# Two token tiles normalised together in the transition of a gated mixer with a grouped mixture of experts

## The chip, the cores and the metric

The kernel runs on one NeuronCore of a Trainium2 chip. The metric is the device time of one execution in microseconds (us), as the median of several runs. A NeuronCore has TensorE (matrix products and transposes, with weight loads of their own), VectorE, ScalarE, GpSimd and SyncE, each with its own queue of instructions that is worked in order. The engines wait for one another by semaphores. TensorE reads SBUF and writes PSUM, whose eight banks hold 512 float32 columns each.

## The reference, cut to what matters

There are 512 tokens of width 1024 and one layer, all in float32. The first half mixes tokens and ends in `w_out`; the second half sends each token to two of 16 experts. Between the two stands a norm:

```python
x = x + g_m * (merged @ w_out)                        # residual
hf = rmsnorm(x, norm_ffn_g) * (1 + sc_f) + sh_f       # norm and modulation
logits = hf @ router_w                                # 16 experts
probs = softmax(logits); best group of 4, best 2 experts in it
x = x + g_f * grouped_moe(hf)                         # gate, up, down of the chosen experts
out = rmsnorm(x, final_norm_g)
```

`rmsnorm(x, g)` is `x * rsqrt(mean(x * x) + 1e-6) * g`, for each token.

## The kernel before, in words

Tokens lie on the 128 partitions, in four tiles (`NT = 4`). Every wide product is made of three, in float32r, from operands split into a high and a low part (`three`, L1203 to L1205). ScalarE makes the high part, VectorE the low part (`lo`, L684); for the first two expert chunks GpSimd makes the low part (L448). A stage of products with `w_out` is followed by the transition, and that by the expert stage, in which expert tiles of up to 128 gathered rows run through one loop. The expert stage starts only when the router's choice is known: VectorE ranks the experts, TensorE and VectorE turn the choice into row numbers, GpSimd gathers rows from a copy of `hf` in DRAM.

The transition is the part that the change touches. The order of each engine's work there is written out by hand:

- **TensorE** finishes `w_out` for tile t in two halves of 512 columns (PSUM bank `4 - 4 * half + t`), tile by tile. After the last half it transposes the normed tiles 0 and 1 (`turn_normed`, L1411), makes the router's logits of both (`logits`, L1400), then transposes tile 2, makes its logits, and the same for tile 3. The transposes of tile t wait for `hf_ready` above t.
- **VectorE** does for each half `mixed(t, half)`: it waits for that half of `w_out`, multiplies it in PSUM by the gate row (L923) and adds `x` into SBUF (L926, `x2_half`). `normed(t)` waits for the sum of squares (`sq2`), takes an inverse root of one column in ten small instructions (`inv_rms_1`, L719 to L729) and scales the tile (L932, `hf_scaled`). The order is: residuals of tile 0, norm 0, residual 1 first half; then, for t from 1 to 3: second half of t, first half of t + 1, norm of t. Last it adds the shift to tile 3 (L956), after GpSimd has added it to tiles 0 to 2 (`hf_ready` at least 3).
- **ScalarE** squares and sums tile t when both halves of its residual are there (L604), and copies transposes from PSUM to SBUF as the router's operand (`turned`, L230). It squares tiles 0, 1, 2, copies transposes 0 and 1, squares tile 3, and copies transposes 2 and 3.
- **GpSimd** adds the shift to tiles 0 to 2 as each is scaled (L454).
- **SyncE** saves each finished tile of `hf` to DRAM (L337), and when all are saved and transposed starts three weight loads for the experts.

`inv_rms(col, n)`, used elsewhere in the kernel for four columns at once, is an inverse root for n columns in twelve dependent small instructions (L695 to L707). After each the engine waits for its end. The loop that orders residuals and norms is:

```python
            for t in range(1, NT):
                mixed(t, 1)
                if t < NT - 1:
                    mixed(t + 1, 0)
                normed(t)
```

Of the kernel before, what the change touches and what calls it, by code (L numbers as in the profile page):

```python
# [15 lines left out]
NT = SEQ // P  # L16
# [28 lines left out]
def tokens_moe_kernel(nc, A, out):  # L45
# [18 lines left out]
    with ctx:  # L64
# [41 lines left out]
        with nc.sbuf_tensor("hT", [P, 2, ND, SEQ], F32R) as hT:  # L106
# [56 lines left out]
        sq2, hf_scaled, hf_ready, hf_saved, hf_t, hfT_ready, logits_mm, expd, mask_ready, pos_mm, tiles_ready = map(  # L163
            sem, ("sq2", "hf_scaled", "hf_ready", "hf_saved", "hf_t", "hfT_ready", "logits_mm", "expd", "mask_ready",
                  "pos_mm", "tiles_ready"))
# [58 lines left out]
        def turned(act, activation, t):  # L224

            for half in range(2):
                act.wait_ge(hf_t, 2 * t + half + 1)
                if t >= 2:
                    act.wait_ge(logits_mm, t - 1)
                activation(hfT[:, t % 2, 4 * half:4 * half + 4, :].rearrange("p k m -> p (k m)"),  # L230
                           ps[:, 5 * (t % 2) + half, :], ACT.Copy).then_inc(hfT_ready, 1)
# [251 lines left out]
        def _(act):  # L483
            A_ = nc.scalar.activation
# [112 lines left out]
                hi(c + 2, c + 2, 16 * (RAW_O // 4 + 2), G0 + 16)  # L597

            for t in range(NT):
                if t == NT - 1:  # L600
                    turned(act, A_, 0)
                    turned(act, A_, 1)
                act.wait_ge(x2_half, 2 * t + 2)
                A_(hf[:, t, :], x_tiles[:, t, :], ACT.Square, accum_out=stats[:, 24 + t:25 + t]).then_inc(sq2, 1)  # L604
            for t in range(2, NT):
                turned(act, A_, t)
            act.wait_ge(sub_ready, 1)
            A_(r_p, r_d, ACT.Exp).then_inc(expd, 1)
# [61 lines left out]
        def _(dve):  # L670
# [3 lines left out]
            def step(ins):  # L674

                steps[0] += 1
                ins.then_inc(chain, 1)

            def done():
                dve.wait_ge(chain, steps[0])  # L680
# [10 lines left out]
            def inv_rms(col, n):  # L691

                m, yv, sq = stats[:, col:col + n], nrm[:, 0:n], nrm[:, NT:NT + n]
                yi, mi = nrm[:, 0:n].bitcast(I32), m.bitcast(I32)
                step(V.tensor_scalar(m, m, 1.0 / D, EPS, ALU.mult, ALU.add))  # L695
                done()

                step(V.tensor_scalar(yi, mi, 1, None, ALU.logical_shift_right))
                done()
                step(V.tensor_scalar(yi, yi, -1.0, float(0x5F3759DF), ALU.mult, ALU.add))  # L700
                done()
                for last in (False, False, True):
                    step(V.tensor_tensor(sq, yv, yv, ALU.mult))
                    done()
                    step(V.scalar_tensor_tensor(out=sq, in0=sq, scalar=-0.5, in1=m, op0=ALU.mult, op1=ALU.mult))
                    done()
                    step(V.scalar_tensor_tensor(out=m if last else yv, in0=sq, scalar=1.5, in1=yv,  # L707
                                                op0=ALU.add, op1=ALU.mult))
                    done()

            def inv_rms_1(col):


                m, z = stats[:, col:col + 1], nrm[:, 0:1]
                zi = z.bitcast(I32)
                powers = [nrm[:, NT + j:NT + j + 1] for j in range(3)]
                for j in range(3):
                    f = 4.0 ** (3 - j)
                    step(V.tensor_scalar(powers[j], m, f / D, f * EPS, ALU.mult, ALU.add))  # L719
                done()  # L720

                step(V.tensor_scalar(zi, powers[2].bitcast(I32), -0.5,
                                     float(0x5F3759DF - (2 << 23) - (1 << 31)), ALU.mult, ALU.add))
                done()
                for j in range(3):
                    step(V.scalar_tensor_tensor(out=nrm[:, 2 * NT:2 * NT + 1], in0=z, scalar=powers[j], in1=z,  # L726
                                                op0=ALU.mult, op1=ALU.mult))
                    done()
                    step(V.scalar_tensor_tensor(out=m if j == 2 else z, in0=nrm[:, 2 * NT:2 * NT + 1],  # L729
                                                scalar=-3.0, in1=z, op0=ALU.add, op1=ALU.mult))  # L730
                    done()
# [188 lines left out]
            def residual(t, half):  # L920

                b = 4 - 4 * half + t
                step(V.tensor_tensor(ps[:, b, :], ps[:, b, :], gm[:, half * 512:half * 512 + 512], ALU.mult))  # L923
                done()
                x_h = x_tiles[:, t, half * 512:half * 512 + 512]
                V.tensor_tensor(x_h, ps[:, b, :], x_h, ALU.add).then_inc(x2_half, 1)  # L926

            def normed(t):

                dve.wait_ge(sq2, t + 1)  # L930
                inv_rms_1(24 + t)
                V.scalar_tensor_tensor(out=hf[:, t, :], in0=x_tiles[:, t, :], scalar=stats[:, 24 + t:25 + t],  # L932
                                       in1=gff, op0=ALU.mult, op1=ALU.mult).then_inc(hf_scaled, 1)

            lo_n(O0 + 3, 3)
            def mixed(t, half):

                if t < NT - 1:
                    dve.wait_ge(o_tile, 2 * t + half + 1)
                else:  # L940
                    dve.wait_ge(chunk_used, M0 - 1 + half)
                residual(t, half)


            mixed(0, 0)
            mixed(0, 1)
            normed(0)
            mixed(1, 0)
            for t in range(1, NT):
                mixed(t, 1)  # L950
                if t < NT - 1:
                    mixed(t + 1, 0)
                normed(t)
            dve.wait_ge(hf_scaled, NT)
            dve.wait_ge(hf_ready, NT - 1)
            V.tensor_tensor(hf[:, NT - 1, :], hf[:, NT - 1, :], shf, ALU.add).then_inc(hf_ready, 1)  # L956
# [575 lines left out]
```

## Time and profile before

| | |
|---|---|
| median of 3 runs | 844.06 us (842.86 to 845.45) |
| span of the profiled execution | 839.1 us |
| its own time beside the span | not given by the page |
| mean granted TensorE clock | 0.951 of full speed |
| TensorE products busy | 760.3 us, 91% of the span |
| VectorE busy | 609.8 us, 73% |
| ScalarE busy | 370.5 us, 44% |
| GpSimd busy | 192.3 us, 23% |

The span runs from the first instruction to the last of one execution. The shares are means over the whole kernel. The transition lies at about 416 to 452 us; there, and up to 477 us, the page shows the only stretch in the middle of the kernel with a lower TensorE clock. In a timeline each row is a group of like instructions one after the other: start, length, engine, line, operation, output and input, count, and in brackets the idle time before it with what ended it.

### The profile page before, as it was taken

How to read it: one execution, taken by the hardware profiler on the slowest of the kernel's cores; microseconds unless marked ns; L12 is line 12 of the kernel's file. 1: busy time of each engine (PE TensorE's matmuls, PEld its weight loads, DVE VectorE, ACT ScalarE, POOL GpSimd, SP SyncE). 2: the span in 40 equal slices, each digit the busy share in tenths (PEclk: the TensorE clock that was granted, in tenths of full speed). 3: DMA queues.
4: the chain of work that ended last, by engine and by line, in shares of the span. 5: the costliest groups of instructions: out<-in, count | busy, mean ns of one | idle time of the engine just before them, and what ended most of it. 6: DMA issues, size and time to landing. Idle time of an engine off the chain costs nothing. (4 is left out here: it accounts for less than half of the span.)

```text
span 839.1 us, 10842 instructions
## 1 busy us (share of the span) xinstructions
PE 760.3 (91%) x3463; PEld 607.4 (72%) x3464; DVE 609.8 (73%) x818; ACT 370.5 (44%) x325; POOL 192.3 (23%) x73
## 2 busy tenths in 40 slices
PE   3989999999999999999996689999999999999910
PEld 1468888866888888886885578888888888888710
DVE  4972343765474757667385799999999999999528
ACT  3142333332322232313324377677677777676301
POOL 1000000401000000000250004554444555554022
PEclk9889999999999999999995699999999999999965
DMA  8963230431365555646445436999999999999052
GB/s 298 329 228 101 95 102 5 151 101 50 102 215 186 183 186 178 202 171 255 151 151 200 143 125 232 342 383 351 350 357 366 360 345 351 346 352 375 28 223 100
DMA packets 108371, 183.93 MB, mean 219 GB/s; under 512 B 7036, under 2 KB 58300, under 8 KB 107836
## 3 DMA queue, kind: packets, MB, share of 16 engines
q1 hardware_dynamic: 101948, 174.62, 59.0%
q0 software_dynamic: 5072, 8.42, 2.7%
q10 hardware_dynamic: 1328, 0.60, 0.3%
q8 instruction: 13, 0.21, 0.1%
q14 instruction: 10, 0.08, 0.0%
HBM read 180.47 MB, written 13.11 MB: 231 GB/s over the span
## 5 line engine op out<-in xcount | busy, mean ns | idle before, releaser
L684 DVE TENSOR_TENSOR wsplit<-raw,wsplit 128x2048 fp32r<-128x2048 f32 x132 | 299.3, 2289 | 94.6 <-ACT wsplit L490 62.1
L632 ACT ACTIVATE wsplit<-raw 128x2048 fp32r<-128x2048 f32 x96 | 184.0, 1920 | 82.9 <-PE ps L1205 82.9
L440 POOL DMA_INDIRECT expert_rows<-work,dest_now x17 | 110.3, 6486 | 143.0 <-DVE work L1137 143.0
L1203 PE MATMUL ps<-wsplit,hgT 128*128 128x512 f32 x272 | 109.5, 403 | 4.7 <-DVE hgT L1056 4.7
L1205 PE MATMUL ps<-wsplit,hgT 128*128 128x512 f32 x272 | 107.9, 397 | 0.0
L1204 PE MATMUL ps<-wsplit,hgT 128*128 128x512 f32 x272 | 107.9, 397 | 0.0
L1203 PE MATMUL ps<-hT,wsplit 128*128 128x512 f32 x256 | 102.3, 400 | 1.0 <-DVE mx L814 1.0
L1205 PE MATMUL ps<-hT,wsplit 128*128 128x512 f32 x256 | 101.1, 395 | 0.0
L1204 PE MATMUL ps<-hT,wsplit 128*128 128x512 f32 x256 | 101.0, 395 | 0.0
L736 DVE SCALAR_TENSOR_TENSOR raw<-raw,c_silu 128x256 f32 (+1 forms) x128 | 62.0, 485 | 16.4 <-DMA raw<-in_w_ada 12.4
L1203 PEld LDWEIGHTS ps<-wsplit,hgT 128*128 128x128 f32 x272 | 51.5, 189 | 16.9 <-DVE hgT L1056 5.4
L1205 PEld LDWEIGHTS ps<-wsplit,hgT 128*128 128x128 f32 x272 | 51.4, 189 | 12.4
L1204 PEld LDWEIGHTS ps<-wsplit,hgT 128*128 128x128 f32 x272 | 51.6, 190 | 11.7
L1203 PEld LDWEIGHTS ps<-hT,wsplit 128*128 128x128 f32 x256 | 48.1, 188 | 13.1 <-issue 1.9
L1204 PEld LDWEIGHTS ps<-hT,wsplit 128*128 128x128 f32 x256 | 48.1, 188 | 12.0 <-issue 0.7
L1205 PEld LDWEIGHTS ps<-hT,wsplit 128*128 128x128 f32 x256 | 48.1, 188 | 11.4
L1203 PE MATMUL ps<-wsplit,aT 128*128 128x512 f32 x136 | 55.0, 405 | 1.5 <-DVE aT L1123 1.5
L448 POOL TENSOR_TENSOR wsplit<-raw,wsplit 128x2048 fp32r<-128x2048 f32 x2 | 9.2, 4622 | 203.0 <-ACT wsplit L490 203.0
L490 ACT ACTIVATE wsplit<-raw 128x2048 fp32r<-128x2048 f32 x20 | 38.2, 1915 | 39.0 <-PE ps L1205 22.5
L1205 PE MATMUL ps<-wsplit,aT 128*128 128x512 f32 x136 | 53.8, 396 | 0.0
L1203 PE MATMUL ps<-wsplit,hT 128*128 128x512 f32 x128 | 52.0, 406 | 1.9 <-DVE hT L780 1.2
L1204 PE MATMUL ps<-wsplit,aT 128*128 128x512 f32 x136 | 53.6, 394 | 0.0
(226 smaller groups left out, 1196.6 us busy)
## 6 DMA issues: line engine op xcount, KB each, us to landing
raw<-in_w_exp_gate SPq DMA_DIRECT2D x32, 1024.0 KB
raw<-in_w_exp_up SPq DMA_DIRECT2D x32, 1024.0 KB
raw<-in_w_exp_down SPq DMA_DIRECT2D x32, 1024.0 KB
raw<-in_w_ada SPq DMA_DIRECT2D x24, 1024.0 KB
raw<-in_w_in SPq DMA_DIRECT2D x20, 1024.0 KB
raw<-in_w_branch_a SPq DMA_DIRECT2D x4, 1024.0 KB
raw<-in_w_branch_b SPq DMA_DIRECT2D x4, 1024.0 KB
raw<-in_w_out SPq DMA_DIRECT2D x4, 1024.0 KB
```

The costliest lines, as they stand in the source:

```text
L440: g.indirect_dma_start(out=y_dram, out_offset=bass.IndirectOffsetOnAxis(ap=dest_now[:, 0:1], axis=0), in_=y, in_offset=None, bounds_check= ...
L448: g.tensor_tensor(wsplit[:, c + 2, 1, :], raw[:, c + 2, :], wsplit[:, c + 2, 0, :].bitcast(F32), ALU.subtract).then_inc(lo_ready, 1)
L490: A_(wsplit[:, n, 0, :], raw[:, slot, :], ACT.Copy).then_inc(hi_ready, 1)
L632: A_(wsplit[:, c, 0, :], raw[:, c, :], ACT.Copy).then_inc(hi_ready, 1)
L684: V.tensor_tensor(wsplit[:, n, 1, :], raw[:, slot, :], wsplit[:, n, 0, :].bitcast(F32), ALU.subtract).then_inc(lo_ready, 1)
L736: ins = V.scalar_tensor_tensor(out=acc, in0=raw[:, slot, k * CC:(k + 1) * CC], scalar=c_silu[:, k:k + 1], in1=acc, op0=ALU.mult, op1=ALU.add)
L1203: nc.tensor.matmul(out, w_hi, m_hi_, start=first, stop=False)
L1204: nc.tensor.matmul(out, w_hi, m_lo_, start=False, stop=False)
L1205: return nc.tensor.matmul(out, w_lo, m_hi_, start=False, stop=last)
```

## The change

VectorE no longer norms tile 2 ahead of the last half residual. It finishes all residuals, waits for the squares of tiles 2 and 3, takes one inverse root for both columns with `inv_rms(26, 2)`, and scales tile 2 and tile 3 one after the other. ScalarE squares all four tiles first and then copies all transposes. The queues of TensorE, GpSimd and SyncE are as they were.

```diff
             for t in range(NT):
-                if t == NT - 1:
-                    turned(act, A_, 0)
-                    turned(act, A_, 1)
                 act.wait_ge(x2_half, 2 * t + 2)
                 A_(hf[:, t, :], x_tiles[:, t, :], ACT.Square, accum_out=stats[:, 24 + t:25 + t]).then_inc(sq2, 1)
-            for t in range(2, NT):
+            for t in range(NT):
                 turned(act, A_, t)
...
                 dve.wait_ge(sq2, t + 1)
                 inv_rms_1(24 + t)
+                scaled_row(t)
+
+            def scaled_row(t):
+
                 V.scalar_tensor_tensor(out=hf[:, t, :], in0=x_tiles[:, t, :], scalar=stats[:, 24 + t:25 + t],
                                        in1=gff, op0=ALU.mult, op1=ALU.mult).then_inc(hf_scaled, 1)
...
             mixed(0, 1)
             normed(0)
             mixed(1, 0)
-            for t in range(1, NT):
-                mixed(t, 1)
-                if t < NT - 1:
-                    mixed(t + 1, 0)
-                normed(t)
+            mixed(1, 1)
+            mixed(2, 0)
+            normed(1)
+            mixed(2, 1)
+            mixed(3, 0)
+            mixed(3, 1)
+            dve.wait_ge(sq2, NT)
+            inv_rms(26, 2)
+            scaled_row(2)
+            scaled_row(3)
             dve.wait_ge(hf_scaled, NT)
             dve.wait_ge(hf_ready, NT - 1)
             V.tensor_tensor(hf[:, NT - 1, :], hf[:, NT - 1, :], shf, ALU.add).then_inc(hf_ready, 1)
```

## Rows read from the trace of the kernel before

**Rows 1.** Windows, one of the expert loop: PE busy, PEld, DVE, ACT, POOL, clock, DMA share, GB/s

```profile
558.00:577.00 19.00, 19.00 (x94) 15.69 (x93) 18.26 (x19) 13.46 (x10) 9.86 (x3) 1.00 1.03 384
```

**Rows 2.** Timeline of TensorE's products in the transition: start us, length us, then the group

```profile
435.71 0.40 PE L1205 MATMUL ps<-wsplit,hT 128*128 128x512 f32 x1
435.94 1.91 PE L1411 MATMUL ps<-ident,raw 128*128 128x128 f32 x16
437.69 3.64 PE L1400 MATMUL ps<-router,work 128*128 128x16 f32 x32
441.61 1.09 PE L1411 MATMUL ps<-ident,raw 128*128 128x128 f32 x8 [0.27 <-POOL raw L454]
442.95 3.29 PE L1400 MATMUL ps<-router,work 128*128 128x16 f32 x16 [0.25 <-ACT work L230]
446.11 1.97 PE L1411 MATMUL ps<-ident,raw 128*128 128x128 f32 x8
447.91 3.59 PE L1400 MATMUL ps<-router,work 128*128 128x16 f32 x16
```

**Rows 3.** Timeline of VectorE in the transition

```profile
422.55 1.41 DVE L726 SCALAR_TENSOR_TENSOR nrm<-nrm 128x1 f32<-128x1 f32 x1
...
435.99 0.27 DVE L719 TENSOR_SCALAR nrm<-stats 128x1 f32<-128x1 f32 x3
...
437.83 1.28 DVE L932 SCALAR_TENSOR_TENSOR raw<-mx,stats,raw 128x1024 f32<-128x1024 f32 x1
439.03 0.69 DVE L923 TENSOR_TENSOR ps<-ps,tmp 128x512 f32<-128x512 f32 x1
439.75 0.69 DVE L926 TENSOR_TENSOR mx<-ps,mx 128x512 f32<-128x512 f32 x1
441.66 0.27 DVE L719 TENSOR_SCALAR nrm<-stats 128x1 f32<-128x1 f32 x3 [1.22 <-ACT raw L604]
...
444.83 1.22 DVE L956 TENSOR_TENSOR raw<-raw 128x1024 f32<-128x1024 f32 x1
```

**Rows 4.** Timeline of GpSimd, transition and tail

```profile
419.32 4.63 POOL L448 TENSOR_TENSOR wsplit<-raw,wsplit 128x2048 fp32r<-128x2048 f32 x1 [0.28 <-ACT wsplit L490]
...
439.19 2.36 POOL L454 TENSOR_TENSOR raw<-raw 128x1024 f32<-128x1024 f32 x1 [3.29 <-DVE raw L932]
...
813.63 8.10 POOL L475 TENSOR_TENSOR raw<-raw 128x1024 f32<-128x1024 f32 x3 [9.96 <-DMA raw<-expert_rows]
```

**Rows 5.** Windows of half a microsecond, where the clock falls (columns as in rows 1)

```profile
443.00:443.50 0.50, 0.50 (x4) 0.50 (x5) 0.40 (x3) 0.38 (x1) 0.00 (x0) 0.82 0.95 393
```

**Rows 6.** Timeline of ScalarE in the transition

```profile
436.58 2.07 ACT L230 ACTIVATE work<-ps 128x512 f32<-128x512 f32 x4 [0.65 <-PE ps L1411]
440.48 1.06 ACT L604 ACTIVATE raw<-mx 128x1024 f32<-128x1024 f32 x1 [1.83 <-DVE mx L926]
```

**Rows 7.** Timeline of VectorE, the four-column inverse root near the start

```profile
17.35 0.17 DVE L695 TENSOR_SCALAR stats<-stats 128x4 f32<-128x4 f32 x1 [3.33 <-ACT raw L500]
...
19.74 2.74 DVE L761 TENSOR_SCALAR mx<-mx,stats 128x1024 f32<-128x1024 f32 x4
```

**Rows 8.** Timeline of VectorE in the tail, beside GpSimd's additions

```profile
816.00 1.23 DVE L1188 TENSOR_TENSOR mx<-mx,raw 128x1024 f32<-128x1024 f32 x1 [2.70 <-POOL raw L475]
...
817.63 1.82 DVE L726 SCALAR_TENSOR_TENSOR nrm<-nrm 128x1 f32<-128x1 f32 x1
...
821.78 0.22 DVE L726 SCALAR_TENSOR_TENSOR nrm<-nrm 128x1 f32<-128x1 f32 x1
```

**Rows 9.** Timeline of TensorE, two places where work sets in at the lower clock

```profile
22.17 5.93 PE L1222 MATMUL ps<-raw,c_silu 128*1 128x256 f32 x16 [3.13 <-DMA raw<-in_w_ada]
...
474.18 0.79 PE L1203 MATMUL ps<-wsplit,hgT 128*128 128x512 f32 x1 [2.37 <-DVE hgT L1056]
```

**Rows 10.** Windows where the clock comes back (columns as in rows 1)

```profile
26.50:27.00 0.50, 0.50 (x3) 0.14 (x2) 0.50 (x1) 0.00 (x0) 0.00 (x0) 0.61 1.11 352
...
477.00:477.50 0.50, 0.50 (x3) 0.40 (x2) 0.50 (x1) 0.50 (x1) 0.00 (x0) 0.55 0.00 0
```

## The prediction

> **What bounds the kernel now.** I read the windows by stage first. In a stretch of the expert loop TensorE is busy for all of its 19.00 us at the full clock [rows 1], so time lost before the loop is not won back inside it: whatever makes the first expert tile late makes the end late. The chain of waits, read next, says the same and reaches back through the expert stage to the row selection, which hangs on the router's result. So the question is when the router logits of the last token tile are finished.
>
> For that I read the timelines of the transition, engine by engine. On TensorE [rows 2]: the last wide product starts at 435.71 and ends at 436.11; then come the transposes of tiles 0 and 1, logits 0 and 1 (3.64 us for the two, 1.82 each), transposes of tile 2 from 441.61, its logits, transposes of tile 3 from 446.11, its logits from 447.91 to 451.50. VectorE waits for that end. From 441.61 to 451.50 TensorE waits for almost nothing. Two things hold this stretch: the start of tile 2's transposes, released by GpSimd's addition that ends at 439.19 + 2.36 = 441.55 [rows 4], and the rate of TensorE's narrow work. Its granted clock fell from 2.4 to 1.2 GHz just after 443.00 (mean 0.82 in that half microsecond) [rows 5], 7 us after the last wide product, and stayed low.
>
> VectorE works with hardly a gap from the norm of tile 0 until 440.44 and is behind: the second half residual of tile 3 runs only at 439.03, though its product was done at 436.11 [rows 2, 3].
>
> **The change part by part.**
>
> 1. The norm of tile 2 (root and scaling, 435.99 to 439.03) leaves its place ahead of the last half residual [rows 3]. That residual is then bound by its product: start 436.11 + 0.03 = 436.14, length 439.03 to 439.75 + 0.69 = 1.41, end 437.55. It is 2.9 us earlier.
>
> 2. ScalarE squares tile 3 at once: start 437.59. From the start of a square to VectorE's first root instruction it took 441.66 - 440.48 = 1.18 [rows 3, 6]. So both sums are known at 438.77.
>
> 3. In ScalarE's queue the copies of transposes 0 and 1 now stand behind that square. They began at 436.58 and took 2.07 for four, 0.52 apart [rows 6]; now the first runs from 438.75 to 439.35. Logits 0 run from 439.4, logits 1 from 441.2, end 443.05 instead of 441.33. TensorE, next in order, would then wait for tile 2 anyway. Cost 0; the cover is that wait, 2.9 us long (below), and without it the cost would be 1.7.
>
> 4. Two one-column roots become one two-column root in the other form: twelve dependent steps. The four-column form took 17.35 to 19.74, 2.39 us [rows 7]; two columns can be no slower, and the one-column root (435.99 to 437.83, 1.84 us [rows 3]) is the lower bound. Since each step is a small instruction whose length is mostly fixed, I take 2.39: scaling of tile 2 starts at 438.77 + 2.39 = 441.16. VectorE saves 2 x 1.84 - 2.39 = 1.29 us of work, but tile 2's scaling, which stood at 437.83, is **3.3 us later**: it now waits for tile 3's residual, square and a longer root.
>
> 5. The scaling of tile 2 ends at 441.16 + 1.28 = 442.44. The scaling of tile 3 stands right behind it; one followed such a scaling after 1.20 [rows 3], so it starts at 442.36. GpSimd's addition of tile 2 is released at about 442.5 and meets it. Here a port matters. While GpSimd's three additions of the tail ran (813.63 to 821.73), a small VectorE step that reads only SBUF and normally takes 0.22 took 1.82 [rows 4, 8]. In the transition such a step took 1.41, from 422.55 to 423.96, and GpSimd's subtraction ended at 423.95 [rows 3, 4]. And the other way: three additions at 2.36 are 7.08, but took 8.10, with a VectorE addition with two SBUF inputs at 816.00 among them [rows 4, 8]. So whichever starts first keeps the other out, and such an addition cost GpSimd 1.02. Here GpSimd loses to a scaling that also reads two SBUF tensors: it begins at about 442.36 + 1.02 plus 0.05 for the longer instruction plus handover, 443.5, rather than 442.5. The price is about 0.95; bounds 0 and 1.28 (the whole scaling). The addition ends at 445.86. The Trainium skill, SBUF — State Buffer, section "Who interferes with whom", states this rule: a VectorE instruction with two SBUF inputs contends with a GpSimd instruction that reads SBUF, and the earlier one holds the port for its whole length; by it the residuals, with one operand in PSUM, left GpSimd alone before and the scaling will not. The trace agrees: the addition at 439.19 ran beside the last half residual and took 2.36 [rows 3, 4].
>
> 6. Transposes of tile 2 start 0.06 after the addition, at 445.92 instead of 441.61: **+4.3**. By then 9.8 us have passed since the last wide product, and TensorE has even done less; I take the clock as low. At the low clock transposes and logits of one tile took 446.11 to 451.50, 5.39, and the next tile's transposes begin 0.13 before the logits end (442.95 + 3.29 = 446.24 against 446.11) [rows 2]: 5.26 per tile. Before, with the clock full for part of it, it was 446.11 - 441.61 = 4.50. So the low clock costs **0.76** more, and tile 3's transposes start at 451.18 instead of 446.11.
>
> 7. Tile 3's own addition on VectorE waits for tile 2's on GpSimd: start 445.9, end 447.1, against a start of 444.83 before. It costs 0 because TensorE is still on tile 2 until 451.2; without that cover, 1.1.
>
> 8. Tile 3's transposes and logits are as before, at the same clock, so logits end at 456.57 against 451.50. SyncE saves rows of tiles 2 and 3 later; its next three weight loads wait for the last transposes, so they move with the chain. The router's arithmetic, selection and gathers move as they are.
>
> 9. Wide work starts again 5.1 us later. Before, it began at 474.18 and the clock came back at about 477.45 (mean 0.55 in the half microsecond from 477.00), 3.3 us later; near the kernel's start a rise came 4.7 us after work began at 22.17 (mean 0.61 from 26.50 to 27.00) [rows 9, 10]. At the low clock work goes at half rate, so the bounds are a gain of 1.6 (no slow stretch) and a loss of 0.7. I take 0.
>
> Sum: 4.31 + 0.76 = **+5.07 us**. The profiled execution spans 839.1; the page gives no other time of it, and the median of the three runs shown is 844.06, 5.0 above, for launch and for what this execution was faster. On the span I expect 844.2, on the median 849.1. A measurement of this kernel can tell about 0.3%, 2.5 us.
>
> **The rivals.**
>
> - **The clock holds (not slower).** If TensorE stays at 2.4 GHz through both tiles, each takes near 3.2: from the start of transposes to that of the logits 442.95 - 441.61 = 1.34, then 1.82. From 445.92 that gives an end near 452.2: +0.7, 844.8. It decides as soon as the fall comes after the last transposes, about 449. For it: the fall came as late as 7 us after the last wide product. Against: now TensorE is idle twice more, for 1.7 and 2.9 us, before tile 2. Chance 0.08.
> - **The clock falls early.** If it falls near 440, logits 0 and 1 take 3.6 each and end near 446.5; they then hold tile 2 instead of GpSimd, 0.6 later: +5.7, 849.8. For it: TensorE is idle from 437.69 to 439.4 where it was not. Chance 0.14.
> - **No wait for the port.** GpSimd adds beside the scaling: 0.9 less, +4.2, 848.2. Against it are the stretched rows. Chance 0.10.
> - **The delay is absorbed later**, in a wait for a weight load in the first expert tiles that used to end last. The loads hang on the same chain, and TensorE's first wide product waits for VectorE, not for a load [rows 9]. 0, 844.1. Chance 0.05.
> - That the change doesn't do what it says: it does, the norms are merged; that this saves VectorE work is true and beside the path.
>
> **How the numbers follow.** The forecast has 0.63. The range must hold forecast, early fall and no port wait (0.87). Low: other executions of before may have had the clock fall before 441.6, which makes before 0.8 slower and the difference smaller; with no port wait 3.4, and half of the runs' spread around it, 846.2. High: 5.7 + 0.7 for the regained clock, and a little spread: 850.8. Slower by over 2.5 us: the three cases, 0.87, less 0.04 for their lower ends, 0.83. Faster needs the clock held and no slow stretch later: 0.02. Same: 0.15.
>
> **What would show it.** VectorE: last half residual at 436.1, a gap of about 1.2, root of twelve steps of 0.16 to 0.17, two scalings back to back. ScalarE: fourth square ahead of the copies. GpSimd: its third addition ends near 445.9, its row longer than 2.41 or its start later than 0.1 after the scaling. TensorE: idle before tile 2's transposes at 445.9, clock 0.50 from then on, logits end near 456.6, everything after shifted alike. It is wrong if the clock is 1.00 in tile 2's logits, if the third addition ends at 445.0, or if the expert stage starts under 4 us later.

## The result and the profile after

The changed kernel takes 848.58 us in the median (848.07 to 850.23, four runs) against 843.46 (842.11 to 845.45, four runs, three of them those shown before). The ratio is 1.0066, interval 1.0048 to 1.0084: slower by 5.1 us, as forecast. The profiled execution spans 846.3 us; its own time is 848.07, so 1.8 us lie around the span.

The timeline of TensorE after, the narrow work of the transition (compare [rows 2]):

```profile
436.67 1.91 PE L1417 MATMUL ps<-ident,raw 128*128 128x128 f32 x16
440.01 4.64 PE L1406 MATMUL ps<-router,work 128*128 128x16 f32 x32 [1.44 <-ACT work L230]
446.61 1.97 PE L1417 MATMUL ps<-ident,raw 128*128 128x128 f32 x8 [1.96 <-POOL raw L454]
448.41 3.59 PE L1406 MATMUL ps<-router,work 128*128 128x16 f32 x16
451.85 1.95 PE L1417 MATMUL ps<-ident,raw 128*128 128x128 f32 x8
453.63 3.59 PE L1406 MATMUL ps<-router,work 128*128 128x16 f32 x16
```

I measure the **transition** from the start of the transposes of tiles 0 and 1 to the end of tile 3's logits: 451.50 - 435.94 = 15.56 us before, 457.22 - 436.67 = 20.55 after. That is 4.99 more. Tile 2's transposes start 9.94 us into it instead of 5.67, released now as before by GpSimd's addition. TensorE is idle ahead of logits 0, which was new, and ahead of tile 2.

The timelines of VectorE, ScalarE and GpSimd after (compare [rows 3, 4, 6]):

```profile
436.87 0.70 DVE L920 TENSOR_TENSOR ps<-ps,tmp 128x512 f32<-128x512 f32 x1
437.60 0.69 DVE L923 TENSOR_TENSOR mx<-ps,mx 128x512 f32<-128x512 f32 x1
439.51 0.17 DVE L692 TENSOR_SCALAR stats<-stats 128x2 f32<-128x2 f32 x1 [1.22 <-ACT raw L601]
...
441.88 2.48 DVE L933 SCALAR_TENSOR_TENSOR raw<-mx,stats,raw 128x1024 f32<-128x1024 f32 x2
446.66 1.22 DVE L962 TENSOR_TENSOR raw<-raw 128x1024 f32<-128x1024 f32 x1 [2.30 <-POOL raw L454]
```

```profile
438.32 1.06 ACT L601 ACTIVATE raw<-mx 128x1024 f32<-128x1024 f32 x1 [1.62 <-DVE mx L923]
...
439.38 2.04 ACT L230 ACTIVATE work<-ps 128x512 f32<-128x512 f32 x4
```

```profile
434.26 2.41 POOL L454 TENSOR_TENSOR raw<-raw 128x1024 f32<-128x1024 f32 x1 [4.56 <-DVE raw L933]
443.24 3.31 POOL L454 TENSOR_TENSOR raw<-raw 128x1024 f32<-128x1024 f32 x1 [6.57 <-DVE raw L933]
```

The last half residual is early, a square and a joint root follow, the two scalings stand back to back, and GpSimd's third addition takes 3.31 us instead of 2.36. The root took 441.88 - 439.51 = 2.37.

The two profiled spans differ by 7.2 us, 2.1 more than the medians. The rest of the timelines tells where. 0.73 us are there before the transition begins (436.67 against 435.94); most of it arose near the kernel's start, where the granted clock was 0.50 under the first wide products until 53.5 us, instead of 50.8. At the end, two things differ in the granted clock. Windows after (the fall in the transition, then the one near the second expert tile), and a timeline of TensorE after, where the first and the second expert tile set in:

```profile
442.50:443.00 0.50, 0.50 (x5) 0.50 (x5) 0.50 (x1) 0.00 (x0) 0.00 (x0) 0.64 0.00 0
...
497.00:497.50 0.50, 0.03 (x1) 0.03 (x1) 0.41 (x1) 0.50 (x2) 0.14 (x1) 0.75 0.00 0
497.50:498.00 0.50, 0.50 (x1) 0.46 (x2) 0.42 (x1) 0.50 (x2) 0.00 (x0) 0.50 0.14 9
```

```profile
479.83 0.80 PE L1209 MATMUL ps<-wsplit,hgT 128*128 128x512 f32 x1 [2.37 <-DVE hgT L1062]
497.47 0.79 PE L1209 MATMUL ps<-wsplit,hgT 128*128 128x512 f32 x1 [2.34 <-DVE hgT L1062]
498.06 0.63 PE L1210 MATMUL ps<-wsplit,hgT 128*128 128x512 f32 x1
```

The second expert tile in the kernel before:

```profile
491.59 0.50 PE L1203 MATMUL ps<-wsplit,hgT 128*128 128x512 f32 x1 [2.35 <-DVE hgT L1056]
```

The first wide product of the expert stage starts at 479.83 against 474.18, 5.65 later: the 0.73, and 4.92 of the transition and the router. At the second expert tile (497.47 against 491.59) it is 5.88. There the clock fell a second time, in a wait of TensorE that the kernel before has too; its row there is 0.50 us long, not 0.79. This is 1.5 us more by the last product (807.41 against 800.04, 7.37 later). So 5.0 of the 7.2 us are the change in the transition. The rest goes with the granted clock elsewhere, in two single executions.

### The profile page after: what moved, and what is told of

Same layout as the page of the kernel before. It is cut to its first block and busy times, and to the rows that moved or that the text cites. A ratio compares the mean times of both kernels' runs of the same rounds, so it can differ in the third digit from the quotient of the medians.

```text
span 846.3 us, 10834 instructions
## 1 busy us (share of the span) xinstructions
PE 763.9 (90%) x3463; PEld 611.2 (72%) x3464; DVE 608.7 (72%) x810; ACT 370.1 (44%) x325; POOL 193.2 (23%) x73
```

## The experiments

All ratios are to the kernel before, run beside them on the same chip. The transition is read as above, from one profiled execution each.

**VectorE's part alone.** The edit puts back ScalarE's order:

```diff
+                if t == NT - 1:
+                    turned(act, A_, 0)
+                    turned(act, A_, 1)
                 act.wait_ge(x2_half, 2 * t + 2)
```

> VectorE's part of the change alone; ScalarE squares tile 3 after the copies of transposes 0 and 1, as before. Measure: the transition, from the start of the transposes of tiles 0 and 1 to the end of tile 3's logits (15.56 us before, 20.55 after). My theory (the late scaling of tile 2 sets it): the fourth square starts when the copies end, about 1.06 later than after the change, and everything follows: 21.6, so some 6 us slower than before in all. Rival (the copies that stand late in ScalarE's queue make logits 0 and 1 late, and those set it): shorter than 20.55.

Median 850.3, ratio 1.0083 (1.0058 to 1.0107), transition 458.20 - 436.73 = 21.47. In its timelines of ScalarE and TensorE:

```profile
437.36 2.06 ACT L230 ACTIVATE work<-ps 128x512 f32<-128x512 f32 x4 [0.90 <-PE ps L1420]
439.29 1.08 ACT L604 ACTIVATE raw<-mx 128x1024 f32<-128x1024 f32 x1
```

```profile
447.59 1.97 PE L1420 MATMUL ps<-ident,raw 128*128 128x128 f32 x8 [5.00 <-POOL raw L454]
...
454.61 3.59 PE L1409 MATMUL ps<-router,work 128*128 128x16 f32 x16
```

The square waits for the copies, and tile 2 with it: logits 0 and 1 are done early and TensorE then idles for 5.00 us. The forecast of 21.6 holds; the rival, that late logits 0 and 1 set the end, is out. The total, 6.2 us over the kernel before, is the forecast 6 too. Within the full change, ScalarE's new order is what saves about 0.9 us.

**ScalarE's part alone.** VectorE as before, with ScalarE squaring all tiles first:

```diff
             for t in range(NT):
-                if t == NT - 1:
-                    turned(act, A_, 0)
-                    turned(act, A_, 1)
                 act.wait_ge(x2_half, 2 * t + 2)
```

> ScalarE's part alone; VectorE norms tile 2 ahead of the last half residual, as before. My theory: now nothing covers the copies: they wait for a residual that ends 4.3 us after the transposes began, logits 0 and 1 end near 446 to 448 on the clock of before and hold tile 2, whose addition was done at 441.55: transition 20.6 with the full clock for logits 0 and 1, up to 23 with the low one. Rival (squaring first is free, as it was in the full change): 15.6.

Median 851.63, ratio 1.0091 (1.0062 to 1.012), transition 460.28 - 436.86 = 23.42. The timeline of TensorE:

```profile
442.85 7.01 PE L1397 MATMUL ps<-router,work 128*128 128x16 f32 x32 [4.09 <-ACT work L230]
449.70 1.95 PE L1408 MATMUL ps<-ident,raw 128*128 128x128 f32 x8
```

Logits 0 and 1 wait 4.09 us for their copies, then take 7.01 at the low clock, and tile 2 follows them without a gap though GpSimd had finished at 442.24. The cover named in step 3 of the prediction is real: with the residual late, the same edit costs 7.6 us in the median (851.63 - 844.08). The transition came out slightly above the upper end I gave, 23.

**GpSimd first at the port.** The changed kernel with one wait more:

```diff
             scaled_row(2)
+            dve.wait_ge(hf_ready, NT - 1)
             scaled_row(3)
```

> The changed kernel with one more wait: VectorE scales tile 3 only after GpSimd has added to tile 2. Port theory: GpSimd's third addition takes 2.36 instead of 3.31 us, tile 2's transposes start 0.95 earlier, transition 19.6; tile 3's addition ends 2.3 us later than in the changed kernel but is covered by TensorE's work on tile 2. Rival (the 3.31 us have another cause, or tile 3 is the one that matters): the row stays at 3.3, or the transition grows to 22.9 or so.

Median 847.5, ratio 1.004 (1.0021 to 1.0059), transition 456.09 - 436.08 = 20.01. Timelines of GpSimd and of TensorE:

```profile
442.67 2.34 POOL L454 TENSOR_TENSOR raw<-raw 128x1024 f32<-128x1024 f32 x1 [6.45 <-DVE raw L933]
```

```profile
439.44 6.23 PE L1407 MATMUL ps<-router,work 128*128 128x16 f32 x32 [1.45 <-ACT work L230]
445.51 1.95 PE L1418 MATMUL ps<-ident,raw 128*128 128x128 f32 x8
```

The addition took 2.34 instead of 3.31 and ended 8.93 us into the transition instead of 9.88. So the scaling beside it is what made the addition longer. Whether a shared port is the means is taken up at step 5 below. The gain did not reach tile 2 in full, because in this execution the clock fell about 4.2 us into the transition (5.97 after the change), logits 0 and 1 took 6.23 us and held tile 2's transposes to 9.43. This is the early fall of the prediction's second rival, met here. In the median the gain is not separated: the intervals of this build and of the changed kernel overlap.

**Two roots instead of one.** All residuals first and ScalarE as changed:

```diff
-            dve.wait_ge(sq2, NT)
-            inv_rms(26, 2)
-            scaled_row(2)
-            scaled_row(3)
+            normed(2)
+            normed(3)
```

> All residuals first and ScalarE squares first, as changed, but two one-column roots: tile 2 is normed while ScalarE squares tile 3. My theory (the delay is the wait of tile 2 for tile 3's square and the joint root, plus the port): tile 2's transposes start about 2.8 us earlier than in the changed kernel, bound now by GpSimd's addition and by logits 1; the small root steps of tile 3 wait for GpSimd (one row near 2 us) but are covered: transition 17.9, total 2.3 us over before. Rival (moving the last half residual ahead of norm 2 is the cost, merging is not): as the changed kernel, 20.5.

Median 846.35, ratio 1.0035 (1.0021 to 1.0048), 2.3 us over before as forecast. Timelines of VectorE, GpSimd and TensorE:

```profile
437.83 0.27 DVE L716 TENSOR_SCALAR nrm<-stats 128x1 f32<-128x1 f32 x3
...
439.66 1.28 DVE L933 SCALAR_TENSOR_TENSOR raw<-mx,stats,raw 128x1024 f32<-128x1024 f32 x1
...
441.16 0.15 DVE L719 TENSOR_SCALAR nrm<-nrm 128x1 int32<-128x1 int32 x1
441.35 2.03 DVE L723 SCALAR_TENSOR_TENSOR nrm<-nrm 128x1 f32<-128x1 f32 x1
```

```profile
441.02 2.35 POOL L454 TENSOR_TENSOR raw<-raw 128x1024 f32<-128x1024 f32 x1 [5.34 <-DVE raw L933]
```

```profile
439.63 6.09 PE L1404 MATMUL ps<-router,work 128*128 128x16 f32 x32 [1.43 <-ACT work L230]
445.56 1.95 PE L1415 MATMUL ps<-ident,raw 128*128 128x128 f32 x8
```

Tile 2's root now fits into the time of tile 3's square, GpSimd meets no scaling, and its addition ends 7.08 us into the transition, 2.80 earlier than in the changed kernel, as expected. Of that, 1.84 is the earlier start (4.73 against 6.57) and 0.96 the shorter row. Tile 3's root pays for it: a step of 0.22 takes 2.03, until GpSimd ends at 443.37. The step ahead of it, with one input, ran beside the same addition and took its usual 0.15. In the profiled execution the early clock hid most of the gain: tile 2's transposes start only 0.67 earlier and the transition is 19.86, not 17.9. Over twelve runs the median is the forecast one. So about half of the change's 0.66% is the merging of the norms, with the meeting at the port that it brings; the other half is what stays with the residual ahead of norm 2 and ScalarE's order. The two intervals touch at 1.0048, so the split is no finer than that, and the transition of the one profiled execution (19.86, near the rival's 20.5) does not show it: the earlier addition does.

**VectorE adds to tile 2.**

```diff
             scaled_row(2)
+            dve.wait_ge(hf_scaled, NT - 1)
+            dve.wait_ge(hf_ready, NT - 2)
+            V.tensor_tensor(hf[:, 2, :], hf[:, 2, :], shf, ALU.add).then_inc(hf_ready, 1)
             scaled_row(3)
```

with GpSimd's loop one tile shorter.

> The changed kernel, but VectorE adds the shift to tile 2 itself, between the two scalings; GpSimd adds to tiles 0 and 1 only. My theory (tile 2's path sets the end): the addition takes 1.22 us and ends 2.2 us earlier than in the changed kernel, so tile 2's transposes start at 7.7 us after those of tiles 0 and 1 instead of 9.9, unless the clock falls so early that logits 1 are later; transition 18.4, with the early fall up to 20. Rival (tile 3's addition, now 46.0 against 45.9 before plus one more wait, decides): 20.5 as after the change.

Median 846.78, ratio 1.0035 (1.0018 to 1.0051), transition 456.40 - 436.64 = 19.76. The timeline of VectorE:

```profile
443.18 1.23 DVE L961 TENSOR_TENSOR raw<-raw 128x1024 f32<-128x1024 f32 x1
444.32 1.28 DVE L933 SCALAR_TENSOR_TENSOR raw<-mx,stats,raw 128x1024 f32<-128x1024 f32 x1
```

The addition ends 7.77 us into the transition, as expected; logits 1, slowed by an early fall again, held tile 2 to 9.18. The rival is out: tile 3's addition ended 10.21 us into the transition and TensorE came to tile 3 at 14.39. The transition lies inside what was expected, near the end given for an early fall; no total had been put down. In the medians the gain over the changed kernel is again not separated.

**The clock held in the transition.** Step 6 of the prediction put the later tiles at the low clock. To take the clock away I gave TensorE wide products with no use, into a PSUM bank that is free, while it waits (calls of `hold(0)`, which issue no product, are left out):

```diff
+            def hold(n, bank=7):
+                pe.wait_ge(lo_ready, M0 + 1)
+                pe.wait_ge(x2_half, 7)
+                for _ in range(n):
+                    nc.tensor.matmul(ps[:, bank, :], wsplit[:, 2, 0, 0:P], wsplit[:, 2, 0, 0:512],
+                                     start=True, stop=True)
...
             turn_normed(0)
             turn_normed(1)
+            hold(6)
             logits(0)
             logits(1)
-            for t in range(2, NT):
-                turn_normed(t)
-                logits(t)
+            hold(11)
+            turn_normed(2)
+            hold(1)
+            logits(2)
+            turn_normed(3)
+            hold(1)
+            logits(3)
```

> The changed kernel with extra wide products on TensorE whose result nobody reads: 6 before logits 0, 11 before tile 2's transposes, 1 ahead of the logits of tiles 2 and 3 each. They fill waits. Clock theory: the clock stays full through tiles 2 and 3, each takes near 3.2 us instead of 5.26 and 5.39, transition 16.5 instead of 20.55, total some 4 us below the changed kernel, near the kernel before. Rival (the narrow work is not slower for the clock, its time is a fixed cost of each instruction): transition 20.5 or more, total no better than the changed kernel.

Median 845.22, ratio 1.0015 (1.0002 to 1.0029), and 3.4 below the changed kernel's median above, which was not measured beside it, transition 454.03 - 436.50 = 17.53. Timeline of TensorE and one window:

```profile
447.40 1.29 PE L1417 MATMUL ps<-ident,raw 128*128 128x128 f32 x8
448.45 0.48 PE L1426 MATMUL ps<-wsplit 128*128 128x512 f32 x1
448.94 1.96 PE L1406 MATMUL ps<-router,work 128*128 128x16 f32 x16
450.75 1.07 PE L1417 MATMUL ps<-ident,raw 128*128 128x128 f32 x8
```

```profile
448.50:454.00 5.50, 5.47 (x44) 4.77 (x42) 0.00 (x0) 3.25 (x5) 0.00 (x0) 1.00 0.37 123
```

At the full clock the logits of a tile take 1.96 us, not 3.59, and a tile 450.75 - 447.40 = 3.35, not 5.24. The narrow work does go with the clock. The products could not keep the clock up (it fell at 444.5 during them and was back by 448.0), and they held tile 2 back by 1.0 us (447.40 - 436.50 = 10.90 against 9.94), so the transition is 1.0 longer than I expected.

**The clock held to the expert stage, with both orders.** The same products in the kernel before (3 between logits 0 and 1, 1 before logits 2, 3 before tile 3's transposes, 1 before logits 3, 27 during the ranking, 6, 6, 9 and 8 around the selections and the gathered rows):

> The kernel before with such products in the waits of TensorE from the transition to the first expert tile: 8 in the transition, 27 during the ranking, 6, 6, 9 and 8 around the selection and the gather. Theory: from tile 3's transposes to the first wide product everything that TensorE does on the chain runs at the full clock: 2.0 less in tile 3, 0.9 each in the prefix product, the first selection and the gathered rows' transposes, 1.6 at the start of the first expert tile: 6.3 us less in all, ratio near 0.9925. Rival (the clock is a small part, or the extra products push the chain back): 1.000 or above.

Median 836.05 over eleven runs, ratio 0.9922 (0.9896 to 0.9947); the forecast was 0.9925, or 6.3 us. The runs spread from 833.87 to 844.01, so that their median lies 8.3 us under that of the kernel before and their mean 6.1. In the profiled one, at 840.82, the clock had fallen to 0.50 by 443 us in spite of the products, stayed there until 460, and the 27 products took 8.99 us; its transition is 454.61 - 436.59 = 18.02, longer than that of the kernel before:

```profile
444.35 3.43 PE L1400 MATMUL ps<-router,work 128*128 128x16 f32 x16
...
451.18 3.43 PE L1400 MATMUL ps<-router,work 128*128 128x16 f32 x16
454.44 8.99 PE L1420 MATMUL ps<-wsplit 128*128 128x512 f32 x27
```

And in the changed kernel:

> The changed kernel held in the same way throughout. Theory: with the clock out of it, what the change costs is the later start of tile 2 less TensorE's slack ahead of tile 3 in the kernel before: logits 3 end 2.9 us later than in the same build of the kernel before. Rival (most of the change's cost was the clock): under 1 us later.

Median 840.33, ratio 0.9954 (0.9941 to 0.9968): 4.3 us over the median of the build of the kernel before, not 2.9, but the two intervals overlap and the size stays open. Nor does the profiled pair decide, since the clock had fallen early in that build (17.54 here against its 18.02). Its timeline of TensorE:

```profile
447.36 1.44 PE L1417 MATMUL ps<-ident,raw 128*128 128x128 f32 x8
...
452.18 1.96 PE L1406 MATMUL ps<-router,work 128*128 128x16 f32 x16
```

The transition is 454.14 - 436.60 = 17.54. The two builds further below that keep the order of before, with other products in the transition, have the full clock up to tile 3's logits: 14.96 and 14.89. That is 2.6 less, near the 2.9 expected. Two things in it are not the change: the eleven products held tile 2 back by 0.8 here (447.36 - 436.60 = 10.76), and tile 3's logits took 3.21 and 3.43 there, not 1.96. Without both it would be about 3.0 to 3.3, an estimate from these rows. That speaks against the rival, that most of the cost was the clock; it was found after the fact, between builds whose products differ.

**Where the gain is.** Products only after logits 3, none in the transition:

> The kernel before with extra wide products only after tile 3's logits (27, 6, 6, 9, 8), none inside the transition. Clock theory: the transition is as before; the clock comes back during the 27 products, and the prefix product, the first selection, the gathered rows' transposes and the first expert tile gain 0.9, 0.9, 0.9 and 1.6: 4.3 us less than before, 0.995, and less scatter from run to run than with products in the transition too. Rival (the gain of 8 us came from the transition): under 1 us.

Median 839.53 (838.79 to 840.15), ratio 0.9949 (0.9929 to 0.9968), 4.0 under the kernel before against 4.3 expected, and with little scatter. Its transition is that of the kernel before, and shows what an early fall does to that: 453.08 - 436.31 = 16.77 against 15.56.

```profile
438.05 4.47 PE L1400 MATMUL ps<-router,work 128*128 128x16 f32 x32
...
452.92 8.66 PE L1420 MATMUL ps<-wsplit 128*128 128x512 f32 x27
461.42 0.34 PE L1440 MATMUL ps<-work,before 128*128 128x80 f32 x2
```

The 27 products, the first of them at the low clock, took 8.66 where the wait is 6.9: the prefix product came 8.34 us after logits 3, not 6.88 as before.

**More products early.** 3 ahead of logits 0, 3 between logits 0 and 1, none ahead of tile 3's transposes:

> As the held build of the kernel before, but 3 products ahead of logits 0, 3 between logits 0 and 1, none ahead of tile 3's transposes. If six products early keep the clock up, tiles 2 and 3 are full-rate in every run: median at or under 836 and no runs above 840. If the fall is set by the narrow logits whatever stands between them, the times split in two groups as before, and the median is 836 to 838.

Median 838.87 (835.36 to 839.2), ratio 0.9929 (0.9906 to 0.9952). In the profile tiles 2 and part of 3 ran at the full clock (transition 451.37 - 436.41 = 14.96). No run is above 840, but the median misses 836. Neither expectation holds as written; whether six products are worth more than three stays open.

**Fewer products during the ranking**, 20 instead of 27, with and without those in the transition:

> The held build with 3, 3, 1 and 1 products in the transition, but 20 instead of 27 during the ranking. With 27 they took 8.4 us where the wait is 6.9, so the prefix product came 1.3 us late. Theory: 20 take at most 6.9 when the first ones run at the low clock; the prefix product is on time and the time falls by about 1.3: median 837.5. Rival (they didn't hold it back, or fewer products fail to raise the clock): 838.9 or more.

> No products in the transition, 20 during the ranking and 6, 6, 9, 8 after it. As with 27, less the 1.5 us by which the prefix product was late there: median 838.1, ratio 0.993. Rival: 839.5 or more.

With 3, 3, 1 and 1 in the transition: 838.32, ratio 0.9939 (0.9922 to 0.9956), transition 451.56 - 436.67 = 14.89, the total between the two expectations and no decision. Without any: 837.8 (837.15 to 839.79), ratio 0.9936 (0.9923 to 0.995), as expected. Its timeline of TensorE:

```profile
452.42 6.11 PE L1420 MATMUL ps<-wsplit 128*128 128x512 f32 x20
459.45 0.45 PE L1440 MATMUL ps<-work,before 128*128 128x80 f32 x2 [0.92 <-DVE work L1015]
...
468.93 1.10 PE L1461 MATMUL ps<-ident,work 128*128 128x128 f32 x8 [0.86 <-DMA work<-hf_rows,tok_idx]
```

The prefix product is on time again, 6.87 us after logits 3, waiting for VectorE and not for TensorE, and the gathered rows' transposes take 1.10 instead of 1.97. In the medians 20 and 27 are not separated (0.9936 and 0.9949, with intervals that overlap); what speaks for 20 is the trace. This is the version to keep of those tried: the order of the kernel before, 49 idle products, 5.4 us (0.6%) under it, with a spread of 2.6 us. The build with 27 and products in the transition too has the lower median (836.05, on another chip) but a spread of 10; with 20, measured beside this one, products in the transition brought nothing (838.32 against 837.8).

## Why the prediction was right

It was right in time (848.58 against 849.1), sign and path. Times below are into the transition, so the 0.73 us ahead of it are out.

| step | forecast | measured |
|---|---|---|
| 1, last half residual starts | 0.20 | 0.20 |
| 2, joint root starts | 2.83 | 2.84 |
| 3, logits 0 start | 3.5 | 3.34 |
| 3, logits 0 and 1 take | 3.64 | 4.64 |
| 3, TensorE idle ahead of tile 2 | 2.9 | 1.96 |
| 4, joint root | 2.39 | 2.37 |
| 5, third addition takes | 2.36 + 0.95 | 3.31 |
| 6, tile 2's transposes start | 9.98 | 9.94 |
| 6, a tile at the low clock | 5.26 | 5.24 |
| 8, logits 3 end | 20.63 | 20.55 |
| sum against before | +5.07 | +4.99 |

- **Steps 1 to 4.** The chain residual, square, joint root, scaling took the place of norm 2. The two-root build shows that the joint root's wait for tile 3, with the port behind it, makes about half of it; the rest stays with the earlier residual and ScalarE's order, not told apart. Step 3 took the full clock for logits 0 and 1. The clock fell within them, so the cover was 1.96 us, not 2.9; it still held.
- **Step 5, the port.** The price was read from a crowded stretch in the tail, 400 us away, and came out to the hundredth, which a price given as "about 0.95" with bounds 0 and 1.28 could not promise. The build that lets GpSimd go first gave the 0.95 back. Of the rule on the port of the Trainium skill, SBUF — State Buffer, section "Who interferes with whom", that the earlier instruction holds it for its length, the trace agrees both ways: GpSimd's row grew to 3.31 behind a scaling, and VectorE's root step to 2.03 behind GpSimd.
- **Step 6, the clock.** It was 0.50 from 443 us on through tiles 2 and 3, as taken. The fall came 6.0 us into the transition, before GpSimd's addition had ended. "The clock holds" is out; "the clock falls early" did not happen in this execution but did in others: 4.2 to 4.7 in five builds. The prediction gave it 0.14 and a price of 0.6. Both were off. It is ordinary scatter, in the kernel before too, where it costs 1.21 (16.77 against 15.56). In the changed kernel it should cost nothing: the build "GpSimd first" has the same TensorE order and started logits 0 at nearly the same point (3.36), its clock fell at 4.24, and TensorE was ready for tile 2 at 9.43, before the 9.94 that GpSimd allows.
- **Step 7.** Tile 3's addition ended 11.2 into the transition, TensorE came to it at 15.2: covered.
- **Step 9.** The regained clock came about 3.8 us after wide work began, against 3.3 before: 0.23 us, inside its bounds. What I did not name is a second fall, in the short wait ahead of the second expert tile, worth 1.5 us in the profiled execution.
- **Delay absorbed later:** out. The delay of 5.65 at the first wide product was 7.37 at the last.

The agreement to 0.1 us is in part luck. The forecast adds the difference against one execution of the kernel before to a median, and that execution was a fast one whose clock fell late: 839.1 and the 1.8 around the span are 840.9, and of the 77 runs of the kernel before beside the experiments, three were as fast. Its transition was 15.56; in the two profiled builds that run the same transition with nothing added, it was 16.77 (fall at 4.4) and 16.16 (fall at 5.1). Against these the changed kernel's 20.55 is 3.8 and 4.4 longer, not 4.99. The prediction had such a fall only in its lower end, at 0.8. The second fall, which seven of the fourteen profiled executions show near the second expert tile, also comes and goes. So sign, path and the steps of one pair of executions are shown; how the 5.1 us between the medians divides is not.

## What to carry to other kernels

Merging the small steps of two tiles makes the first tile wait for the last: count when the first one's consumer starts, not how many instructions are saved. Here 1.3 us less work on VectorE cost 5.1 us of time. Before putting two engines on neighbouring steps, check how many of their operands lie in SBUF: a GpSimd addition behind a two-operand VectorE instruction waits for it, and the reverse is as true. Where TensorE does only narrow work on a serial path between two dense stages, useless wide products in its waits can pay for themselves, if their number fits the wait at the low clock too.

## What the runs showed of the hardware

- The clock fell at quite different points into the narrow work: 7.4 us (before), 6.0 (after), 5.1 and 5.7 in two builds, and 4.2 to 4.7 in five, all without added products in the transition. The kernel before's own transition had it at 7.4, 5.1 and 4.4. With it, and with the wait ahead of them, logits 0 and 1 took from 3.64 to 7.01 us. I had expected a fall at about the same place each time.
- A TensorE wait of 2.35 us ahead of the second expert tile left the clock at 2.4 GHz in one execution and at 1.2 in another, and the latter cost 1.5 us.
- Wide products that nobody reads did not prevent the fall when mixed with narrow logits: it came at 6.3 us with 3 between logits 0 and 1, at 8.0 and 8.2 with 6 before and 11 after them, and at 11.7 and 12.2 with 3 before and 3 between. 20 or 27 in a row after logits 3 brought the clock back in all five profiled executions in which it was down there, and shortened four steps of the router's path.
- GpSimd's addition of 128x1024 took 3.31 us instead of 2.36 with a VectorE scaling that reads two SBUF tensors beside it; a one-column VectorE step with two inputs took 2.03 instead of 0.22 beside such an addition, and the one-input step next to it its usual 0.15.
